# A bidirectional RWKV-7 recurrence on one core: Exps one a step, the store ahead of other loads, three loads spread over seven steps

## The reference

```python
    def step(S, inp):
        r_t, w_t, k_t, v_t, a_t, b_t = inp
        sa = jnp.einsum('zbhvk,zbhk->zbhv', S, a_t)
        S = S * w_t[..., None, :] + sa[..., None] * b_t[..., None, :] + v_t[..., None] * k_t[..., None, :]
        return S, jnp.einsum('zbhvk,zbhk->zbhv', S, r_t)
    ...
    y = ys[0] + jnp.flip(ys[1], axis=1)
    mean = jnp.mean(y, axis=-1, keepdims=True)
    var = jnp.mean((y - mean) ** 2, axis=-1, keepdims=True)
    y = ((y - mean) * lax.rsqrt(var + LNX_EPS)).reshape(B, T, C)
    y = y * lnx_g.astype(f32) + lnx_b.astype(f32)
    bonus = jnp.einsum('bthn,zbthn,hn->bth', r_h, k_dir, r_k.astype(f32))[..., None] * v_h
    return ((y + bonus.reshape(B, T, C)) * g).astype(out_dtype)
```

## Time and profile before

| | |
|---|---|
| runs of the kernel before | median 2936.55 us, 2935.13 to 2938.57 |
| the profiled execution | 2939.54 us |
| its span | 2937.6 us |
| instructions | 44674 |
| TensorE busy | 2819.4 us, 96% |
| VectorE, ScalarE, GpSimd busy | 1381.5, 983.3, 631.8 us |
| DMA | 297.73 MB, mean 101 GB/s |
| mean granted clock of TensorE | 0.986 |

### The profile page before, as it was taken

The page is one execution under the profiler, slowest core; times in us unless marked ns, Lnnn a source line. Parts: engine busy times, 40 slices in busy tenths (PEclk is TensorE's granted clock), DMA queues, the critical chain, the costliest instruction groups (busy, mean ns, idle before and its releaser), DMA issues. The chain is left out here.

```text
span 2937.6 us, 44674 instructions
## 1 busy us (share of the span) xinstructions
PE 2819.4 (96%) x18476; PEld 1760.0 (60%) x18476; DVE 1381.5 (47%) x2307; ACT 983.3 (33%) x1678; POOL 631.8 (22%) x377
## 2 busy tenths in 40 slices
PE   7899999999999999899999998897999999999999
PEld 5566666666666666577777887773544444444443
DVE  3555464656565564577776654554431111112413
ACT  3323242333323232566665676573310000000001
POOL 1132231314041322100000133341143333330000
PEclk9999999999999999899999999998999999999999
DMA  3052534424242525133410567863411111113012
GB/s 96 29 179 90 164 112 126 151 80 158 95 158 73 178 90 162 60 97 84 134 34 10 129 146 180 195 208 109 152 50 43 43 44 48 51 43 129 0 36 86
DMA packets 192505, 297.73 MB, mean 101 GB/s; under 512 B 84480, under 2 KB 119072, under 8 KB 186032
## 3 DMA queue, kind: packets, MB, share of 16 engines
q1 hardware_dynamic: 181936, 252.20, 29.5%
q10 hardware_dynamic: 10368, 42.67, 3.6%
HBM read 188.54 MB, written 106.27 MB: 100 GB/s over the span
## 5 line engine op out<-in xcount | busy, mean ns | idle before, releaser
L637 PE MATMUL pp_ps<-uT,pp_w 128*128 128x347 f32 x3072 | 908.9, 456 | 3.2 <-PEq L190 2.5
L637 PEld LDWEIGHTS pp_ps<-uT,pp_w 128*128 128x128 f32 x3072 | 581.5, 190 | 319.8 <-issue 8.4
L862 POOL TENSOR_TENSOR pp_neighbours<-pp_raw 128x1040 f32<-128x1040 f32 x24 | 46.9, 1954 | 622.9 <-ACT pp_raw L738 622.9
L1441 DVE TENSOR_REDUCE at_mn<-at_S 128x1 f32<-128x1040 f32 x128 | 156.2, 1238 | 47.6 <-PE at_S L1277 47.0
L1277 PE MATMUL at_S<-at_kR,at_qR 64*128 64x512 f32 (+1 forms) x768 | 163.1, 500 | 13.9 <-ACT at_v L1371 5.9
L1340 PE MATMUL at_ob<-at_v,at_pT 128*128 128x128 f32 x1152 | 163.3, 287 | 0.9 <-DVE at_o L1448 0.5
L2300 PE MATMUL fh_b<-u2T,fh_ws 128*128 128x512 f32 x352 | 158.2, 592 | 0.0
L2300 PE MATMUL fh_b<-fh_t,fh_ws 128*128 128x512 f32 x352 | 154.7, 592 | 0.0
L1340 PEld LDWEIGHTS at_ob<-at_v,at_pT 128*128 128x128 f32 x1152 | 139.5, 192 | 17.4 <-DVE at_o L1448 15.7
L1277 PEld LDWEIGHTS at_S<-at_kR,at_qR 64*128 64x128 f32 x768 | 90.4, 189 | 95.8 <-issue 69.0
L1389 ACT ACTIVATE at_p<-at_S,at_mn 128x1040 f32<-128x1040 f32 x128 | 144.5, 1129 | 6.2 <-DVE at_mn L1441 5.7
(11 more groups left out here) (286 smaller groups left out, 4546.2 us busy)
## 6 DMA issues: line engine op xcount, KB each, us to landing
pp_w<-in_w_main SPq DMA_DIRECT2D x64, 512.0 KB, 3.9
s_kept<-pp_ob ACTq DMA_DIRECT2D x48, 520.0 KB, 4.9
fh_w<-in_w_ffn_in SPq DMA_DIRECT2D x44, 512.0 KB, 4.4
rc_kb<-s_kb SPq DMA_DIRECT2D x64, 256.0 KB, 3.9
rc_aw<-s_ar SPq DMA_DIRECT2D x64, 256.0 KB, 4.3
s_ar<-pp_ar SPq DMA_DIRECT2D x8, 1088.0 KB, 4.0
s_kb<-pp_kb SPq DMA_DIRECT2D x8, 1088.0 KB, 7.3
s_vz<-pp_vz SPq DMA_DIRECT2D x8, 1088.0 KB, 9.1
```

The lines of the kernel that those rows point to most:

```text
L637: ins = nc.tensor.matmul(ps[s][:, n, 0:NW], weights, moving[:, n * NW:(n + 1) * NW], start=(k == 0), stop=(k == len(parts) - 1))
L862: nc.gpsimd.tensor_tensor(neighbours[:, real], raw[:, 0:T], raw[:, 2:T + 2], ALU.add).then_inc(once[f"summed_{x}"], 1)
L1441: nc.vector.tensor_reduce(mn[t % 2][:, m:m + 1], S[m][:, 0:T], AX, ALU.min).then_inc(least[m], 1)
```

## The change

Three edits, all in `recurrence`:

- SP: `store(p - 1)` is issued after quarter (1, 3) of round p; before it was issued ahead of quarter (2, 0). Between the two stands `load_ge(p + 1)`, which now follows the store.
- SP: the three `load_kept` of a round are issued after quarters (2, 1), (2, 3) and (3, 1); before after (2, 0), (2, 1) and (2, 2).
- ScalarE: `raise_logs(p - 1, ...)` is called for one piece in each of the steps 5, 6, 7 and 8; before for two in step 5 and two in step 6.

```diff
--- before.py
+++ after.py
@@ -1051,6 +1051,7 @@
 PIECES = [(g, part) for part in ("inner", "outer") for g in range(2)]
 LN = [(what, piece) for pair in ((0, 1), (2, 3)) for what in ("centre", "vary") for piece in pair]
 INNER_AT, OUTER_AT, RAISED_AT = 13, 1, 5
+STORED_AT, KEPT_AT = (1, 3), ((2, 1), (2, 3), (3, 1))
 LNX_EPS = 64e-5
 
 
@@ -1572,13 +1573,13 @@
                 for p in range(ROUNDS):
                     for j in range(NGROUP):
                         n = NGROUP * p + j + HELD
-                        if j == 2 and p > 0:
-                            store(p - 1)
                         for step in range(GROUP):
                             if n < NGROUP * ROUNDS:
                                 load_quarter(n, step)
-                            if j == 2 and p > 0 and step < len(kept):
-                                load_kept(p, list(kept)[step])
+                            if p > 0 and (j, step) == STORED_AT:
+                                store(p - 1)
+                            if p > 0 and (j, step) in KEPT_AT:
+                                load_kept(p, list(kept)[KEPT_AT.index((j, step))])
                         if j == 0 and p + 1 < ROUNDS:
                             load_first(p + 1)
                         if j == 1 and p + 1 < ROUNDS:
@@ -1848,9 +1849,8 @@
                         nc.scalar.copy(yT[p % 2][:, :, SEQ - 1 - c:SEQ - 1 - c - CH:-1], src[:, :, 1, :]).then_inc(y_kept, 1)
                     if normalised_at(q):
                         keep_ln(*normalised_at(q))
-                    if p > 0 and s in (RAISED_AT, RAISED_AT + 1):
-                        for piece in (2 * (s - RAISED_AT), 2 * (s - RAISED_AT) + 1):
-                            raise_logs(p - 1, piece)
+                    if p > 0 and RAISED_AT <= s < RAISED_AT + len(PIECES):
+                        raise_logs(p - 1, s - RAISED_AT)
                 for piece in range(2):
                     raise_logs(ROUNDS - 1, piece)
                 for n in range(4, 6):
```

## The result

The changed kernel took 2956.39 us (median, 2952.49 to 2961.52) against 2935.84 us for the kernel before, with one more run of it: a ratio of 1.0069, 95% interval 1.0051 to 1.0086, so about 20 us slower (15 to 25). The profiled execution of the changed kernel took 2952.49 us, with a span of 2950.6; that is the fastest of its runs, 3.9 us under its median, while the profiled execution of before (2939.54) is 3.7 us above its own. One execution, among the six of the kernel with the gates behind the squares further on, ran at a mean granted clock of 0.747, took 3678.87 us, and isn't counted in any number here.

The account below looks back on a forecast made before the run. TensorE, busy 96% of 2937.6 us, bounds the kernel. Two later passages, 14.6 + 12.4 us with the store's gain inside, less 5.1 for the Exps, give +21.9: 2958.4 from a median of 2936.55, range 2941 to 2968.

Parts of the forecast that it names:

- The mechanism: Starts of rounds 2 and 3: late `gate_r` holds `gates`, the squares and TensorE's product; step 4 begins +14.6 and +12.4 us.
- The wait named in advance: TensorE waits for GpSimd's `rc_sq` 10 to 18 us at the "vary" product, twice; about 8 us if the queue drained.
- The landing: `gate_r` in SP's queue, into rounds 2 and 3: lands 14.0 us later, behind 2432 KB more at 178 GB/s.
- the queue never empties on the way: SP's queue between `gate_r`'s old and new place stays filled; before, `gate_r` took 15.8 and 17.7 us from issue to use.
- rival (1): SP's queue drains between the spread loads; `gate_r` lands 6 to 12 us after issue: +7 us (+1.5 to +13), 2944; chance 0.16.
- Rival (2): Starts of rounds 2 and 3: later `gate_r` is hidden, lighter queue ends the pauses; 18.7 us faster, 2917.8; chance 0.07.
- The pauses of before: TensorE's "issue" pauses, 1.84 and 4.37 us, at the starts of rounds 2 and 3, counted inside passages of 20.71 and 24.46.
- The clock's cost: Starts of rounds 2 and 3: the clock after a TensorE pause adds 2.9 us to each passage.
- rival (3): Clock stays at 1.2 GHz longer after a 17 us pause, or Exps gain only 2.1 us: +30, 2967; chance 0.12.
- The Exps: ScalarE, one Exp in each of steps 5 to 8: 5.1 us gained, 2.1 if the clock still falls in step 6.
- The store: Issued ahead of `load_ge`, it lands earlier for ScalarE's step 13: 1.5 and 1.3 us gained in rounds 1 and 2.

## Why the prediction was right, step by step

**The mechanism was right.** The wait named in advance is there: the "vary" product of piece 2 in step 3 of rounds 2 and 3, released by GpSimd's `rc_sq`, behind `gates`, behind `gate_r`. It was shown by moving each link: the loads alone (+26), their place (+9, +15, +20), and the order on GpSimd (-30). Forecast +21.9 us, measured +20.5 between the medians, so 2958.4 against 2956.39. The mechanism carries the sign and the size; that the two numbers are within 2 us of each other is luck, since terms were off on opposite sides.

**The landing was put too late.** The forecast had `gates` start 17.3 and 18.5 us after the copy of step 1; the two traces of the whole change have 14.8 and 13.4, 17.9 and 12.8, in the mean 14.7. The term that failed is "the queue never empties on the way". It does, between the spread loads, in step 16 of round 1 and in step 14 of round 2. These are windows of the changed kernel (the last columns are clock, DMA share and GB/s):

```profile
1779.00:1780.00 1.00, 1.00 (x23) 0.77 (x20) 0.12 (x1) 0.57 (x2) 0.00 (x0) 1.00 0.05 18
1873.50:1875.00 1.50, 1.50 (x33) 1.26 (x30) 0.91 (x2) 0.67 (x2) 0.00 (x0) 1.00 0.15 39
```

So the transfers issued up to there are through, while the forecast still counted them ahead of `gate_r`; the 0.82 from 1770 to 1780 is the mean over a full queue and this hole. `gate_r` then took 9.5 us from issue to use (1791.49 to 1800.97) and 9.0 (1897.92 to 1906.94), not 12.9. That is rival (1)'s landing, 6 to 12 us after issue, but not its price of +7 us, +13 at the most. Rival (2) falls at the point that it named: `gate_r` had to land by 0.5 us after the copy of step 1, and `gates` began 14.8 and 13.4 us after it.

**The pauses of before were taken as they stood in one trace.** The forecast set the new passages against 20.71 and 24.46 us. The five traces that load at the old places (before, Exps alone, store alone, the gates alone, the loads back at their old places) have 20.71, 17.19, 17.83, 18.93, 17.55 (mean 18.4) in round 2 and 24.46, 19.02, 23.59, 18.37, 24.58 (mean 22.0) in round 3. The trace of before thus holds some 5 us of pauses more than usual. New passages are 35.4 and 32.1 in the mean of two traces; the increase is 17.0 + 10.1 = 27.1 us where the forecast had 36.8 - 20.71 + 38.2 - 24.46 = 29.8. The landing put too late made the forecast 6 us too large, the long pauses of the one trace made it 5 us too small. With the Exps' 3.5 and the 2.0 us by which the wait for the store fell, 27.1 - 3.5 - 2.0 = 21.6 us are near the 20.5 measured.

**The clock's cost** after a wait was put at 2.9 us. In round 2 of the changed kernel 33.35 - 17.19 - 14.18 = 1.98; in round 3 31.89 - 17.19 - 11.26 - 0.25 - 0.59 (two pauses named "issue") = 2.6. Step 3 alone tells it better. In the five traces with the wait (both of the whole change, the loads alone, `gate_r` in step 16 and in step 0) the ten waits are 3.28 to 15.56 us, and what step 3 takes beyond its 5.73 us and the wait is 1.4 to 2.9 us, 2.5 at the shortest wait and 2.9 at the longest. So a longer wait costs no more clock, and rival (3) found nothing to stand on there.

**The Exps** were put at 5.1 us and gave 3.5. The mechanism and the tight 0.70 us gap held. The 1.53 us counted for step 6 of rounds 1 and 3 was too much, as the clock falls there in three cases of ten.

**The store** was put at 2.8 us. The waits became 2.0 us shorter in the mean of the traces, so its mechanism holds, and the store alone showed no gain in time (0.9 us at the most). Its worth stays unconfirmed.

## What to carry to other kernels

When a load is moved to a later place in an in-order queue, ask which wait it releases, and what stands behind that wait on the waiting engine: an operation that needs the load early in a list holds back neighbours that don't. Moving the consumer behind those neighbours turned a loss of 20 us into a gain of 10, with the same transfers. And before a pause in one trace is booked as a gain, look at a second execution of the same work: here the same passages, from step 16 to step 3 of the next round, took 5.7 us more than clean ones in one execution and 11.7 in another.

## What the runs showed of the hardware

TensorE's instructions come by DMA through the same 16 engines as the data. The page of before lists them in a queue of their own (columns: packets, MB, share of 16 engines):

```profile
q8 instruction: 148, 2.42, 0.4%
```

148 packets for 36952 matmuls and weight loads are 250 a packet. That these packets are TensorE's is read from their count and from the pauses. They stay away before TensorE pauses. This is the DMA view of before from 1883.5 to 1893.3 us, which ends within the pause of 4.37 us (1891.99 to 1896.36) that the earlier trace rows shows; `q8` has no line in it, while the kernel's own queue fills the engines:

```profile
q1 hardware_dynamic: 1101, 1.88, 107.1%
q14 instruction: 2, 0.02, 0.7%
```

A packet every 6 to 7 us is what TensorE needs in a passage of 319 matmuls in 17 us; none came for almost 10. The next is in the view from 1893.3 to 1894.8:

```profile
q8 instruction: 1, 0.02, 5.5%
```

It is through at 1894.71, and TensorE goes on at 1896.36, 1.65 us later. So it is everywhere: the fourteen traces hold 53 pauses named "issue" of over 0.15 us in the recurrence, and each ends 1.3 to 1.8 us after the end of a `q8` packet. One of them stands in step 12 of round 0 in every trace, and without the kept loads of rounds 1 and 2 it is the only one left.

The traces don't show what a packet waits for within an engine. So it is open why steps 1 to 3 take 1.8 us more than the clean 17.19 in one trace (Exps alone) and 10.8 in another (before), both rounds together. With steps 16 and 0 it is 5.7 against 11.7, as the trace of Exps alone has a pause of 1.94 us just ahead of step 1.

The Trainium skill, "Runtime: NRT & Kernel Launch", section "Instruction fetch mechanics", has the fetch of instructions hidden because the sequencer issues more slowly than the blocks come. The trace doesn't agree where the engines are full (share 1.07), and the pauses in steps 1 to 3 are gone where it is 0.56 and 0.54.
